# The gate's product with its sigmoid made by GpSimd instead of VectorE in the expert loop of a hybrid decoder step

## The reference

```python
def expert_block(args):
    xb, e = args
    g = xb @ w_gate[e] + b_gate[e]
    u = xb @ w_up[e] + b_up[e]
    g = jnp.minimum(g, SWIGLU_LIMIT)
    u = jnp.clip(u, -SWIGLU_LIMIT, SWIGLU_LIMIT)
    h = (u + 1) * (g * jax.nn.sigmoid(SWIGLU_ALPHA * g))
    return h @ w_down[e] + b_down[e]
```

## Time and profile before

| | us |
|---|---|
| median of 3 runs | 1508.89 (1506.41 to 1509.22) |
| the profiled execution, its own time | 1508.62 |
| its span, first to last instruction | 1506.9 |
| TensorE busy | 1437.8 |
| VectorE busy | 1273.0 |
| ScalarE busy | 1054.8 |
| GpSimd busy | 185.7 |

### The profile page before, as it was taken

The page is one execution under the profiler, slowest core; times in us unless marked ns, Lnnn a source line. Parts: engine busy times, 40 slices in busy tenths (PEclk is TensorE's granted clock), DMA queues, the critical chain, the costliest instruction groups (busy, mean ns, idle before and its releaser), DMA issues.

```text
span 1506.9 us, 21417 instructions
## 1 busy us (share of the span) xinstructions
PE 1437.8 (95%) x7157; PEld 1054.0 (70%) x7157; DVE 1273.0 (84%) x1234; ACT 1054.8 (70%) x961; POOL 185.7 (12%) x192
## 2 busy tenths in 40 slices
PE   6999987879999999999999999999999999999993
PEld 5999766736777777777777777777777777777772
DVE  4344377479999999999999999999999999999995
ACT  4456342447777877778787878787878777787875
POOL 4000140151000111000000000000011100000000
PEclk9999997669999999999999999999999999999997
DMA  7411412169999999999999999999999999999994
GB/s 226 124 57 57 149 54 70 42 244 339 382 379 378 371 374 363 376 369 375 371 377 372 379 372 377 371 374 372 376 372 368 374 362 380 364 364 380 385 357 161
DMA packets 170325, 464.78 MB, mean 308 GB/s; under 512 B 13957, under 2 KB 27921, under 8 KB 170017
## 3 DMA queue, kind: packets, MB, share of 16 engines
q1 hardware_dynamic: 157240, 430.99, 76.8%
q0 software_dynamic: 9072, 24.01, 7.0%
q10 hardware_dynamic: 3976, 9.34, 1.8%
HBM read 447.90 MB, written 23.59 MB: 313 GB/s over the span
## 4 chain that ended last, share of the span: by engine, by line
PE 89%; DVE 4%; DMA 2%; issue 2%; ACT 1%; DVEq 1%; ACTq 1%; POOL 0%; POOLq 0%; SPq 0%
PE ps L1737 85%; PE ps L1740 4%; DMA ring<-in_x_prompt 0%; DMA slot_rows<-reg_t,entry_at 0%; DMA xhat_rows<-reg_w 0%; DMA acc_rows<-reg_a,pass_tok 0%; DVE ring_r L451 0%; ACT ring L1135 0%; DVE reg_w L1465 0%; POOL slot_rows L675 0%; DVE ring_r L1178 0%; DVE ring L1728 0%; ACTq L756 0%; DVE ring L1442 0%; DVE reg_b L1438 0%
## 5 line engine op out<-in xcount | busy, mean ns | idle before, releaser
L1737 PE MATMUL ps<-ring_r,reg_z_r 128*96 128x512 f32 x4608 | 1098.3, 395 | 0.0
L1737 PEld LDWEIGHTS ps<-ring_r,reg_z_r 128*96 128x96 f32 x4608 | 736.8, 162 | 309.6 <-issue 0.4
L1062 ACT ACTIVATE ring_r<-ring 128x2048 fp32r<-128x2048 f32 x387 | 735.9, 1915 | 168.3 <-PE ps L1737 164.2
L451 DVE TENSOR_TENSOR ring_r<-ring,ring_r 128x2048 fp32r<-128x2048 f32 x355 | 797.8, 2284 | 52.0 <-ACT ring_r L1062 51.9
L736 POOL DMA_INDIRECT acc_rows<-reg_a,pass_tok x32 | 49.3, 1542 | 998.9 <-ACT reg_a L1079 932.6
L1737 PE MATMUL ps<-reg_a_r,ring_r 128*128 128x264 f32 (+1 forms) x576 | 110.2, 286 | 0.0
L1737 PE MATMUL ps<-ring_r 128*128 128x256 f32 (+3 forms) x372 | 101.9, 323 | 0.0
L1737 PEld LDWEIGHTS ps<-reg_a_r,ring_r 128*128 128x128 f32 x576 | 90.6, 188 | 2.4 <-issue 2.2
L1085 ACT ACTIVATE reg_z_r<-ps 128x384 fp32r<-128x384 f32 x130 | 59.0, 480 | 38.3 <-PE ps L1740 38.3
L1665 DVE TENSOR_TENSOR ring_r<-ring,ring_r 128x1024 fp32r<-128x1024 f32 x64 | 77.7, 1214 | 0.0
L1737 PEld LDWEIGHTS ps<-ring_r 128*128 128x128 f32 (+1 forms) x372 | 67.7, 184 | 7.7 <-issue 0.5
(11 more groups left out here) (330 smaller groups left out, 926.3 us busy)
## 6 DMA issues: line engine op xcount, KB each, us to landing
ring<-in_w_gate SPq DMA_DIRECT2D x131, 1024.0 KB, 7.5
ring<-in_w_up SPq DMA_DIRECT2D x128, 1024.0 KB, 6.1
ring<-in_w_down SPq DMA_DIRECT2D x128, 1024.0 KB, 8.7
ring<-in_w_in SPq DMA_DIRECT2D x9, 1024.0 KB, 6.7
ring<-in_w_out SPq DMA_DIRECT2D x4, 1024.0 KB, 5.0
ring<-in_x_prompt SPq DMA_DIRECT2D x4, 512.0 KB, 8.9
reg_a<-in_x_prompt SPq DMA_DIRECT2D x4, 512.0 KB, 6.5
xhat_rows<-reg_w ACTq DMA_DIRECT2D x4, 512.0 KB, 2.7
```

What stands on the lines that cost most here:

```text
L451: return eng.tensor_tensor(rest_r(k), w, rounded_r(k).bitcast(F32), ALU.subtract)
L1062: act.activation(rounded_r(k), ring[:, slot_of(k), :], ACT.Copy).then_inc(hi_ready, 1)
L1737: return pe.matmul(out, lhsT, rhs, start=start, stop=stop, skip_group_check=True)
```

## The change

The product moves from VectorE's list to GpSimd's. There it stands at the head of each expert, ahead of the wait for `ex_psum` and the gather, and raises a new semaphore `gate_made`; VectorE waits for that in the place where it made the product. Two semaphores of the start of the kernel, `ident_made` and `masks_made`, become one, `pool_made`, which counts to 2.

```diff
-        ident_made, masks_made, rows_made, iotas_made = sem("ident_made"), sem("masks_made"), sem("rows_made"), sem("iotas_made")
+        rows_made, iotas_made = sem("rows_made"), sem("iotas_made")
+
+        pool_made = sem("pool_made")
+        gate_made = sem("gate_made")
...
-            sp.wait_ge(masks_made, 1)
+            sp.wait_ge(pool_made, 2)
...
-                               channel_multiplier=1).then_inc(ident_made, 1)
+                               channel_multiplier=1).then_inc(pool_made, 1)
...
-                pool.engine_nop().then_inc(masks_made, 1)
+                pool.engine_nop().then_inc(pool_made, 1)
...
                     for e in range(NE):
                         u = e % 2
+                        alone(pool, sg_ready, base + (e + 1))
+                        pool.tensor_tensor(eS[0:CAP, :], eS[0:CAP, :], eG[0:CAP, :], ALU.mult).then_inc(gate_made, 1)
                         alone(pool, ex_psum, base + (e + 1))
                         gather(u, e + 2)
...
-                    dve.wait_ge(masks_made, 1)
+                    dve.wait_ge(pool_made, 2)
...
                             rest_of_piece(k + 7, p12)
-                            dve.wait_ge(sg_ready, t + 1)
-                            dve.tensor_tensor(eS[0:CAP, :], eS[0:CAP, :], eG[0:CAP, :], ALU.mult)
+                            dve.wait_ge(gate_made, t + 1)
                             for q in range(2):
...
-            pe.wait_ge(ident_made, 1)
+            pe.wait_ge(pool_made, 1)
```

## The result

The changed kernel takes 1538.28 us (median of 4 runs, 1536.30 to 1539.02), the kernel before 1507.82 us in the same comparison (4 runs, 1506.41 to 1509.22): a ratio of 1.0201, 95% interval 1.0188 to 1.0213. It is slower by 30.5 us; 1539.5 was forecast, slower by 30.5.

The account below looks back on a forecast made before the run. TensorE, busy 1000 of 1000 us in the expert loop, was taken to set the pace. Losses of 1.3 + 15 x 0.73 + 16 x 1.14 = 30.5 us on the 1508.9 us median gave 1539.5 us, range 1530 to 1552.

Parts of the forecast that it names:

- TensorE sets the pace, nothing can be gained: Expert loop: TensorE busy 1000.00 of 1000.00 us, so freeing VectorE, busy 945.25, cannot by itself gain anything.
- The product is let in at the split's end and ends 2.25 us behind it: GpSimd's product, excluded during VectorE's split of piece k+7, starts at 822.86, not 821.63, and ends at 825.11.
- 0.15 us from there to the clamp: VectorE's register step and second wait between gate_made and the clamp: 0.15 us, with ends 0.05 and 0.30.
- The clamp 1.35 us late: VectorE's clamp starts 2.40 us after the split instead of 1.05, making everything behind it 1.35 us later.
- TensorE's losses: Lateness beyond slack at TensorE's loads: even expert 0.51, 0.73 us in all; odd 1.01, 1.14 in all.
- even expert: One of a pair's two alternating experts, the other being odd; called u=0, but its rows are of u=1.
- 15 experts at 0.73 and 16 at 1.14: Loss summed over the loop's experts after the first: even 15 x 0.73 = 10.9, odd 16 x 1.14 = 18.2 us.
- The first expert pays 1.3 us: First expert of the loop: next to no slack, 0.05 us, so it loses about 1.3 us.
- The gather, the merged semaphore, the clock cost nothing: Gather queued behind the product, pool_made merged, TensorE's clock grant kept despite short stops: nothing added for any.
- A: Rival: GpSimd and VectorE do not exclude each other; clamp 0.3 us later, +2 us, 1511; chance 0.08.
- B: Rival: the gather behind the product takes the port pair and holds hrow 0.30 us, 9.6 in all, 1549; chance 0.12.
- C: Rival: VectorE was the true pace and the product becomes hidden; at most 29 us faster, 1480; chance 0.03.

Follow-up runs that it names:

- no_product: Changed kernel with the product left out altogether; hrow is multiplied with the sigmoid alone and VectorE waits only for the sigmoid: 1507.25 us.
- wait_ahead: Changed kernel with VectorE's wait for gate_made moved ahead of the split of piece k+7, so no VectorE operation runs beside the product: 1582.27 us.
- idle runs: idle_two, idle_copy and idle_memset: VectorE makes the product as before, GpSimd does work nobody waits for; 1566.83, 1522.46 and 1509.25 us.
- gather_first: Changed kernel with the gather back in its old place, ahead of the product on GpSimd: 1537.11 us.
- relay_only: Changed kernel with the product back on VectorE; GpSimd only passes the sigmoid's signal on, the merged semaphore stays: 1507.88 us.
- half_product: Changed kernel with GpSimd's product on the first 512 columns only; the other 512 are multiplied with the plain sigmoid: 1508.29 us.
- split_in_halves: Changed kernel, VectorE splitting half of piece k+7 before the clamp, half behind the hrow operation, and waiting for gate_made only ahead of hrow: 1524.02 us.
- half_each: Changed kernel with VectorE making product columns 0 to 511, GpSimd the rest; gate_made awaited only before hrow's second half: 1512.82 us.
- idle_product: Changed kernel with the product back on VectorE; GpSimd makes an unread product, one constant region as both inputs, at the sigmoid's end: 1546.53 us.
- idle_copy: As idle_product, but GpSimd only copies one 96x1024 region, a single SBUF input: 1522.46 us.
- idle_two: As idle_product, but GpSimd's unread product has two different regions as inputs: 1566.83 us.
- idle_memset: As idle_product, but GpSimd only writes, with two memsets of 96x1024: 1509.25 us.

## Why the prediction was right

- *TensorE sets the pace, nothing can be gained.* Right, and now shown by no_product, which gains nothing.
- *The product is let in at the split's end and ends 2.25 us behind it.* 2.27 us. That it is exclusion, not a slow product, is shown by wait_ahead (2.41 us) and by the three idle runs.
- *0.15 us from there to the clamp.* 0.13 us.
- *The clamp 1.35 us late.* 1.35 us.
- *TensorE's losses.* By the loads: from one expert's bias to its transposes of `hrow` TensorE lost 0.51 us in the even expert (20.35 us before, 20.86 after) and 1.02 in the odd one (20.33, 21.35), forecast 0.51 and 1.01. From there to the next bias it lost 0.16 and 0.15, forecast 0.22 and 0.13. That is 1.84 us per pair against 1.87.
- *15 experts at 0.73 and 16 at 1.14.* The counts are exchanged, because the names were: the first expert is of the kind called odd. The sum should read 1.3 + 16 x 0.73 + 15 x 1.14 = 30.1 us.
- *The first expert pays 1.3 us.* Not seen between the two profiled executions. In that of the changed kernel ScalarE's first roundings came 2 us earlier (the wait on GpSimd's queue ahead of them ended sooner), and its `hrow` was ready at 363.25 instead of 363.92. The rows under this list show why: GpSimd's last DMA issue ahead of the loop started 0.06 us after VectorE's split in the one and 0.11 us ahead of it in the other, and took 2.97 against 0.87 us. In the profiled executions of all 13 kernels it took 2.75 to 2.97 us where it started behind the split's start (4, the kernel before and three with the merged semaphore) and 0.87 where it started ahead (9). So that is a race which falls either way, not the change. It accounts for 2.0 of the 2.8 us by which the profiled executions differ less (27.7 us) than the medians (30.5). The sum's agreement with the medians to a tenth is luck, better than its terms deserve.
- *The gather, the merged semaphore, the clock cost nothing.* Right: gather_first and relay_only, and a grant of 1.00 through the loop.
- *Rivals.* A falls with wait_ahead and the idle runs, B with gather_first, C with no_product. A's price, 2 us for a clamp 0.3 us late, fits what half_product shows: 0.22 us late, 0.4 us more.

The last issue ahead of the loop and VectorE's split, before and after:

```profile
336.03 2.28 DVE L451 TENSOR_TENSOR ring_r<-ring,ring_r 128x2048 fp32r<-128x2048 f32 x1
336.09 2.97 POOL L675 DMA_INDIRECT slot_rows<-reg_t,entry_at  x1 [0.30 <-issue]
...
335.34 0.87 POOL L678 DMA_INDIRECT slot_rows<-reg_t,entry_at  x1 [0.30 <-issue]
335.45 2.28 DVE L454 TENSOR_TENSOR ring_r<-ring,ring_r 128x2048 fp32r<-128x2048 f32 x1
```

Where I was wrong was in the experiment split_in_halves. I took VectorE's start of the clamp as set by its own queue; it coincided, to 0.01 us in the even expert, with TensorE's delivery of the sums. A start that two causes allow at the same moment moves only one way.

None of the variants beats the kernel before, and since TensorE is full there in the loop, none that only moves this product can.

## What to carry to other kernels

Before work is moved from VectorE to GpSimd, look at what VectorE is doing at that moment: if it reads two operands from SBUF, a GpSimd operation that reads SBUF (here a product or a copy) takes turns with it, and the moved work costs its GpSimd length (2.3 us here) in the place where it cost its VectorE length (1.2 us). A memset beside it was free, and so was a VectorE clamp from PSUM beside GpSimd's product. An engine that is 5% idle can still be the one that decides: read the slack at each hand-off, in each variant of the unrolled body, add up lateness minus slack, and the loss follows where the chain is shifted as a whole. And if the engine that sets the pace has no holes, leave the operation out once as a test, before looking for a better place for it.

## What was not expected of the hardware

GpSimd's length under exclusion depends on whether its two inputs are the same region: with one region twice, VectorE's product took 2.91 us and so stood 1.7 us, with two regions 3.45 us in the median and so 2.2.

At a boundary between two back-to-back VectorE operations the waiting GpSimd operation went first in all 32 experts of half_each, idle_product and idle_copy, by the length of VectorE's operation (its shortest and longest lie within 0.02 us there). In idle_two the first expert differs: GpSimd's operation was issued only at 361.67, with VectorE's product already running since 361.25. The product kept its 1.22 us, GpSimd was let in behind it, and the next two-input operation, that of `hrow`, stood instead (2.14 us for 0.69).

The issue of indirect DMAs on GpSimd stands behind VectorE's two-input operations as well. The gather took up to 2.26 us to issue in the kernel before, where splits ran beside it, and about 1.0 us in the changed one, where VectorE was at its clamp; the line's views, before and after (ns, shortest, median, longest):

```profile
L697 POOL DMA_INDIRECT reg_a<-xhat_rows,pass_tok x34: 961/2064/2255, 329.9 to 1450.5; - x34
```

```profile
L700 POOL DMA_INDIRECT reg_a<-xhat_rows,pass_tok x34: 957/1013/1054, 329.2 to 1491.9; - x34
```

In idle_memset it took 4.49 to 4.67 us in all 32 experts, through a split and a half that followed each other without a gap, and in split_in_halves some 7.5 us in every second expert, so at those boundaries it was not let in. In the kernel before it was: 31 gathers ended 0.87 us behind the first of two splits without a gap between them, and the second split still took its 2.28 us. So this issue waits for VectorE but, unlike a computing operation, was not seen to hold it. What decides at which boundary it gets in stays open; no run was made for it.
